# Attention inside a hybrid diffusion backbone: stacked query parts for the scores, values of two units at one visit, transposes behind the branch's weight products

## The reference, cut to what matters

```python
for l in range(DEPTH):                                   # DEPTH = 2
    hx = modulate(rms_norm(x, g_mix[l]), sh1, sc1)       # latent; hc the same of the context
    px = split_cols(hx @ w_in[l], IN_SIZES)              # q, k, v, conv, short conv, Fourier, 4 gates
    q = apply_rope(px[0].reshape(b, s, N_HEADS, HEAD_DIM), cos, sin)      # 8 heads of 64
    k = apply_rope(px[1].reshape(b, s, N_KV_HEADS, HEAD_DIM), cos, sin)   # 2 key heads
    y_attn = windowed_latent_attention(q, k, v, kc, vc, sink)   # window +-128, and all context keys
    m = sum(sigmoid(gate_i) * (y_i @ w_br_i) for the four branches)
    x = x + gt1 * (m @ w_out[l])
    # in layer 0 the context stream does the same, its queries reading the context keys alone
    x = x + gt2 * conv_ffn(...)                          # w_up, depthwise conv, silu, w_down
```

## Time and profile before

| | us |
|---|---|
| median of 3 runs (1251.46 to 1252.34) | 1252.09 |
| the profiled execution's own time | 1252.31 |
| its span, first to last instruction | 1250.5 |

### The profile page before, as it was taken

How to read it: one execution, slowest core, us unless ns; L and a number is a source line. 1 busy time by engine, 2 the same in 40 slices (tenths; PEclk the granted TensorE clock), 3 DMA queues, 4 the chain that set the end, 5 groups by cost and what they waited for, 6 DMA issues and landing times.

```text
span 1250.5 us, 19713 instructions
## 1 busy us (share of the span) xinstructions
PE 1241.1 (99%) x7504; PEld 1074.4 (86%) x7504; DVE 913.3 (73%) x1229; ACT 560.5 (45%) x912; POOL 340.7 (27%) x270
## 2 busy tenths in 40 slices
PE   8999999999999999999999999999999999999998
PEld 6788777787888898888888888899999999998996
DVE  4799889562898777662879674577897566778677
ACT  5223465653423345332223332344676645754554
POOL 1006699110143001111001110003693130144243
PEclk9999999999999999999999999999999999999999
DMA  9666422112466416562555664335433554556553
GB/s 380 221 214 197 147 65 71 65 54 99 143 191 227 136 61 203 186 225 80 182 166 188 212 194 145 122 119 189 150 123 118 175 178 138 186 185 207 180 170 116
DMA packets 52804, 200.33 MB, mean 160 GB/s; under 512 B 6001, under 2 KB 7921, under 8 KB 51569
## 3 DMA queue, kind: packets, MB, share of 16 engines
q1 hardware_dynamic: 52576, 199.13, 48.5%
q10 hardware_dynamic: 144, 0.07, 0.0%
HBM read 196.81 MB, written 1.05 MB: 158 GB/s over the span
## 4 chain that ended last, share of the span: by engine, by line
PE 97%; DVE 1%; ACT 0%; DMA 0%; issue 0%; DVEq 0%
PE psA L640 25%; PE psA L642 25%; PE psA L641 25%; PE psB L642 3%; PE psB L640 3%; PE psB L641 3%; PE psB L993 2%; PE psB L981 2%; PE psB L1140 2%; PE psB L1141 2%; PE psB L1142 2%; PE psA L968 1%; PE psA L646 1%; PE psA L651 1%; PE psA L647 1%; PE psB L675 1%
## 5 line engine op out<-in xcount | busy, mean ns | idle before, releaser
L640 PE MATMUL psA<-h_hi,w_hi 128*128 128x512 f32 (+1 forms) x1448 | 491.5, 339 | 0.1
L642 PE MATMUL psA<-h_hi,w_lo 128*128 128x512 f32 (+1 forms) x1448 | 488.0, 337 | 0.0
L641 PE MATMUL psA<-h_lo,w_hi 128*128 128x512 f32 (+1 forms) x1448 | 487.9, 337 | 0.0
L1196 ACT ACTIVATE w_hi<-raw 128x1024 fp32r<-128x1024 f32 (+2 forms) x246 | 274.2, 1117 | 278.0 <-PE psA L642 166.8
L1565 DVE TENSOR_TENSOR w_lo<-raw,w_hi 128x1024 fp32r<-128x1024 f32 (+2 forms) x246 | 339.4, 1380 | 61.5 <-ACT w_hi L1196 61.0
L640 PEld LDWEIGHTS psA<-h_hi,w_hi 128*128 128x128 f32 x1448 | 274.8, 190 | 29.9 <-DVE w_lo L1565 0.9
L642 PEld LDWEIGHTS psA<-h_hi,w_lo 128*128 128x128 f32 x1448 | 274.8, 190 | 29.1
L641 PEld LDWEIGHTS psA<-h_lo,w_hi 128*128 128x128 f32 x1448 | 274.9, 190 | 28.5 <-issue 0.2
L627 POOL TENSOR_TENSOR hid_lo<-sig,hid_hi 128x512 f32 (+3 forms) x44 | 68.6, 1558 | 441.5 <-ACT hid_hi L1513 441.5
L1597 DVE SCALAR_TENSOR_TENSOR ada_sum<-raw,csil,ada_sum 128x1024 f32<-128x1024 f32 x112 | 156.7, 1430 | 0.0
L2058 DVE SCALAR_TENSOR_TENSOR tmp<-psA,vec,tmp 128x510 f32<-128x510 f32 (+1 forms) x44 | 27.1, 615 | 68.3 <-ACT tmp L1524 68.1
(11 more groups left out here) (246 smaller groups left out, 1814.2 us busy)
## 6 DMA issues: line engine op xcount, KB each, us to landing
raw<-w_up SPq DMA_DIRECT2D x88, 512.0 KB, 4.3
raw<-w_ada SPq DMA_DIRECT2D x80, 512.0 KB, 3.5
raw<-w_in SPq DMA_DIRECT2D x35, 512.0 KB, 4.3
raw<-w_at SPq DMA_DIRECT2D x24, 512.0 KB, 3.5
raw<-w_dn SPq DMA_DIRECT2D x16, 704.0 KB, 5.2
raw<-w_dn SPq DMA_DIRECT2D x22, 512.0 KB, 3.5
raw<-w_fn SPq DMA_DIRECT2D x16, 640.0 KB, 4.1
raw<-w_sc SPq DMA_DIRECT2D x16, 640.0 KB, 3.9
```

Of the source, the lines that this page charges most:

```text
L640: pe.matmul(out, w0, hi, start=first, stop=False)
L641: pe.matmul(out, w0, lo, start=False, stop=False)
L642: return pe.matmul(out, w1, hi, start=False, stop=last)
L1196: act.activation(w_hi[:, s, 0:tiles * P], raw[:, r, 0:tiles * P], ACT.Copy).then_inc(head_done, 1)
```

## The change

The query's parts are stacked: `q_two` holds for each half of the heads the high part in that half's partitions and the low part in the other half's, and `k_two[half]` holds that half's high keys in both halves of the partitions. One matmul of 128 rows then gives q_hi k_hi + q_lo k_hi for a half; q_hi k_lo stays a pair of 64 rows. The band goes between the two kinds. ScalarE writes four copies of 64 partitions for the keys and two for each query; VectorE's subtractions become two of 64 partitions.

Values of units k-1 and k (k odd) are multiplied at one visit, with both units' weights side by side. The transposed weights lie in unused tails of the weight slots (layer 0) or in the context half of `h_hi` (layer 1). The results of two units are split by one instruction. In places below 16 the transposes come behind the branch's weight products, and ScalarE does the exponentials of a place before the copies of its transposes.

```diff
-        q_hi = place("q_hi", [2, P], F32R)
-        q_lo = place("q_lo", [2, P], F32R)
+        q_two = place("q_two", [2, 2, P], F32R)
...
-        k_hi = at("k_hi", [NT], F32R, sqa_off)
+        k_two = [at("k_two0", [NT], F32R, sqa_off), at("k_two1", [NT], F32R, t_off + 4 * NT * 2)]
+        prob_tails = at("prob_tails", [3 * SLOTS, SLOT], F32, base)[:, :, SLOT - P:SLOT]
+        prob_pair = at("prob_pair", [KD, NT], F32, h_off)[:, :, SEQ:NT]
...
+        def two_units(layer, y, unit):
+            _, qi, t = unit
+            if layer:
+                return y[:, 3 + t:5 + t, P * qi:P * qi + P]
+            return y[:, 4 + t, :].rearrange("p (s n) -> p s n", s=2)[:, :, P * qi:P * qi + P]
...
# TensorE, scores(k)
-                    pe.wait_ge(q_rest, b0 + k + 1)
+                    pe.wait_ge(q_rest, 2 * (b0 + k + 1))
                     b = (b0 + k) % 2
+                    for half in range(2):
+                        pe.matmul(score_bank(layer, half)[:, 0:nk * P], q_two[:, b, half, :],
+                                  k_two[half][:, k0 * P:(k0 + nk) * P], start=True, stop=False, skip_group_check=True)
                     if s == 0:
                         for half in range(2):
                             pe.matmul(score_bank(layer, half)[:, (1 - qi) * P:(2 - qi) * P], band[:, 2, :],
-                                      band[:, qi, :], start=True, stop=False, skip_group_check=True)
-                    for part, (qs, ks) in enumerate(((q_hi, k_hi), (q_hi, k_lo), (q_lo, k_hi))):
-                        for half in range(2):
-                            rows = slice(64 * half, 64 * half + 64)
-                            mm = pe.matmul(score_bank(layer, half)[:, 0:nk * P], qs[rows, b, :],
-                                           ks[rows, k0 * P:(k0 + nk) * P], start=(s == 1 and part == 0),
-                                           stop=(part == 2), skip_group_check=(s == 0))
-                            if part == 2:
-                                mm.then_inc(s_mm, 1)
+                                      band[:, qi, :], start=False, stop=False, skip_group_check=True)
+                    for half in range(2):
+                        rows = slice(64 * half, 64 * half + 64)
+                        pe.matmul(score_bank(layer, half)[:, 0:nk * P], q_two[rows, b, half, :],
+                                  k_lo[rows, k0 * P:(k0 + nk) * P], start=False, stop=True, skip_group_check=True)\
+                            .then_inc(s_mm, 1)
...
# TensorE, values(k)
+                    if k % 2 == 0:
+                        return
...
-                    for b in range(nk):
+                    for b in range(4):
+                        n = P if layer == 0 and b < 2 else 2 * P
                         for half in range(2):
-                            mm = pe.matmul(out_bank[64 * half:64 * half + 64, 0:P],
-                                           v[:, k0 + b, 64 * half:64 * half + 64],
-                                           probT[:, half, b * P:(b + 1) * P], start=(b == 0), stop=(b == nk - 1))
-                    mm.then_inc(o_mm, 1)
+                            if layer:
+                                prob = prob_pair[:, 4 * half + b, :]
+                            elif b < 2:
+                                prob = prob_tails[:, 6 * half + b, :]
+                            else:
+                                prob = prob_tails[:, 6 * half + b:6 * half + b + 3:2, :]
+                            mm = pe.matmul(out_bank[64 * half:64 * half + 64, 0:n],
+                                           v[:, b, 64 * half:64 * half + 64],
+                                           prob, start=(b == 0), stop=(b == 3),
+                                           skip_group_check=True)
+                    mm.then_inc(o_mm, 2)
...
# TensorE, attend(place), and at the end of merge
+                    if place >= 16:
+                        turn_place(place)
+
+                def turn_place(place):
                     for k, half in halves_at(layer, place, LATE[layer]["turn"]):
                         turn(k, half)
...
                     mm.then_inc(chunk_done, 1)
+                    if place is not None and place < 16:
+                        turn_place(place)
...
# ScalarE
-                    act.activation(q_hi[:, (b0 + k) % 2, :], q[:, t, q0:q0 + P], ACT.Copy).then_inc(q_head, 1)
+                    for half in range(2):
+                        rows = slice(64 * half, 64 * half + 64)
+                        act.activation(q_two[rows, (b0 + k) % 2, half, :], q[rows, t, q0:q0 + P], ACT.Copy).then_inc(q_head, 1)
...
-                act.activation(k_hi[:, :], k_all[:, :], ACT.Copy).then_inc(k_head, 1)
+                act.wait_ge(evac, n0 + 16)
+                for half in range(2):
+                    for into in range(2):
+                        act.activation(k_two[half][64 * into:64 * into + 64, :], k_all[64 * half:64 * half + 64, :], ACT.Copy)\
+                            .then_inc(k_head, 1)
...
# ScalarE, attend(place): attended, then
+                    for k, half in halves_at(layer, place, 0):
+                        weigh(k, half)
                     for k, half in halves_at(layer, place, LATE[layer]["turn"]):
                         turned(k, half)
-                    for k, half in halves_at(layer, place, 0):
-                        weigh(k, half)
...
# VectorE
-                dve.wait_ge(k_head, layer + 1)
-                dve.tensor_tensor(k_lo[:, :], k_all[:, :], k_hi[:, :].bitcast(F32), ALU.subtract).then_inc(k_rest, 1)
+                    for half in range(2):
+                        rows, others = slice(64 * half, 64 * half + 64), slice(64 - 64 * half, 128 - 64 * half)
+                        dve.tensor_tensor(q_two[others, (b0 + k) % 2, half, :], q[rows, t, q0:q0 + P],
+                                          q_two[rows, (b0 + k) % 2, half, :].bitcast(F32), ALU.subtract).then_inc(q_rest, 1)
+
+                dve.wait_ge(k_head, 4 * (layer + 1))
+                for half in range(2):
+                    rows = slice(64 * half, 64 * half + 64)
+                    dve.tensor_tensor(k_lo[rows, :], k_all[rows, :], k_two[half][rows, :].bitcast(F32), ALU.subtract)\
+                        .then_inc(k_rest, 1)
```

More of the change, by code:

```diff
@@ L275, in program @@
         k_lo = at("k_lo", [NT], F32R, k_off)
-        k_hi = at("k_hi", [NT], F32R, sqa_off)
+        k_two = [at("k_two0", [NT], F32R, sqa_off), at("k_two1", [NT], F32R, t_off + 4 * NT * 2)]
         x_in = at("x_in", [KD, NT], F32, q_off)
+        prob_tails = at("prob_tails", [3 * SLOTS, SLOT], F32, base)[:, :, SLOT - P:SLOT]
+        prob_pair = at("prob_pair", [KD, NT], F32, h_off)[:, :, SEQ:NT]
+        assert all(KD * P <= n * P <= SLOT - P for name, n in (("fn", SIZE[START["fn"]]), ("sc", SIZE[START["sc"]]), ("at", SIZE[START["at"]])))
         ada_first = at("ada_first", [FIRST_SLOTS, KD, 2 * P], F32, y_off)
@@ L952, in scores @@
                     if k == 0:
-                        pe.wait_ge(k_rest, layer + 1)
+                        pe.wait_ge(k_rest, 2 * (layer + 1))
                         pe.wait_ge(v_done, layer + 1)
@@ L985, in values @@
                 def values(k):
[L986 to L987 removed]
+                    if k % 2 == 0:
+                        return
                     pe.wait_ge(pt, 2 * (b0 + k) + 2)
[L989 to L991 removed]
+                    if b0 + k > 1:
+                        pe.wait_ge(o_rest, b0 + k - 1)
+                    for b in range(4):
+                        n = P if layer == 0 and b < 2 else 2 * P
                         for half in range(2):
[L993 to L996 removed]
+                            if layer:
[9 more added lines that the diff above has]
+                    mm.then_inc(o_mm, 2)
                 def attend(place):
@@ L1394, in turned @@
                     act.wait_ge(t_mm, 2 * b + half + 1)
-                    if b:
-                        act.wait_ge(o_mm, b)
-                    act.activation(probT[:, half, 0:wide(layer, k)], turn_bank(layer, half)[:, 0:wide(layer, k)], ACT.Copy)\
+                    if b > 1:
+                        act.wait_ge(o_mm, b - k % 2)
+                    n = wide(layer, k) // P
+                    if layer:
+                        into = prob_pair[:, 4 * half:4 * half + 4, k % 2 * P:(k % 2 + 1) * P]
+                    else:
+                        into = prob_tails[:, 6 * half + 4 * (k % 2):6 * half + 4 * (k % 2) + n, :]
+                    act.activation(into,
+                                   turn_bank(layer, half)[:, 0:n * P].rearrange("p (b n) -> p b n", b=n), ACT.Copy)\
                         .then_inc(pt, 1)
                 def attended(k):
-                    s, qi, t = un[k]
-                    c0 = SEQ * s + P * qi
-                    act.wait_ge(o_mm, b0 + k + 1)
-                    act.activation(y_hi[:, 4 + t, c0:c0 + P], out_bank[:, 0:P], ACT.Copy)\
-                        .then_inc(o_head, 1)
```

(16 more changed lines are left out.)

5 lines of the change are left out of this document (1 added, 4 removed).

## The result

| | before | after |
|---|---|---|
| median, us | 1252.21 (6 runs, 1251.46 to 1253.94) | 1262.11 (6 runs, 1260.55 to 1262.58) |
| ratio, 95% interval | 1 | 1.0076 [1.0065, 1.0086] |
| profiled execution, its span, us | 1252.31, 1250.5 | 1261.99, 1260.2 |

The change costs 9.9 us, 0.8%; the range reached only to 1254.4. TensorE's list of waits answers to the earlier trace rows and already names the places. Columns: engine, tile and line, what it waited for, us in total, times, longest. It is the whole list but one, 0.4 us on a DMA at the start.

The account below looks back on a forecast made before the run. TensorE, busy 99% of the span, was taken to bound the kernel. From 1252.31, less 1.16 gained on TensorE, plus 1.5 at layer 1's start, adjusted to the median and for joined passes: 1252.3 us, range 1249.9 to 1254.4.

Parts of the forecast that it names:

- Stacked products at 0.23: TensorE's scores: two products filling all 128 rows run one after the other, 0.23 us each; scores sum to 0.88, unchanged.
- the pair at 0.42: TensorE's scores: the remaining pair of 64 rows takes 0.42 us from its start to the next product.
- joined passes at half the cost of two: TensorE's values: one matmul over two units streams as long as the two did, 0.22 us; only fixed visit cost goes.
- first transposes behind the products without a switch: TensorE: transposes behind the weight products keep the full shape and pay no switch, 0.11 us each, the first too.
- no wait for the scaled weights: Layer 1: TensorE's 0.40 us wait for the scaled weights goes, as the transposes come 0.7 us later.
- the exponentials covered: ScalarE's exponentials wait for later transposes, but have about 4 us to spare in layer 0 and 2 in layer 1.
- The faster rival: A fixed cost goes with every matmul removed: 1250.5 us, or 1247.9 at about 60 cycles each; chance 0.10.
- The start of layer 1: Before layer 1's first scores, extra key copies and half ops make TensorE wait 1.5 us in the open.
- The upper bound, 2.8: Start of layer 1: the added wait reaches 2.8 us if each half op meets GpSimd.
- In layer 0 the same edit is covered: Start of layer 0: query's low parts ended two microseconds before the first score; extra ops are 0.63 and some 0.6.
- short by up to 0.6: Start of layer 0: if the extra ops met GpSimd twice, the cover would fall short by up to 0.6 us.
- The rival "VectorE falls behind": Layer 0: a second low-part op per place makes VectorE late; at 1.0 a pair it costs 3 us, 1255.3; chance 0.09.

Follow-up runs that it names:

- e1: The changed kernel without its stacked scores; scores and the splits of queries and keys as before, joined values and moved transposes kept: 1251.79 us, ratio 0.9993.
- e8: The changed kernel run once more, unaltered, for a second look at TensorE's clock: 1261.65 us, ratio 1.0073.
- e4: The changed kernel with 14 unused TensorE matmuls added just before it waits for layer 1's first scores: 1259.75 us, ratio 1.0057.
- e3: The kernel before, with only VectorE's subtractions for queries and keys cut into two ops of 64 partitions: 1257.03 us, ratio 1.0037.
- e5: The change with the stack turned round: one VectorE op per query, five ScalarE activations per query, two key copies instead of four: 1252.84 us, ratio 1.0000.
- e7: The changed kernel with ScalarE writing first the two key copies VectorE reads, then the two others from them: 1259.12 us, ratio 1.0054.
- e6: The changed kernel with GpSimd's convolution taps, all but each layer's first, over only 4 columns of each stream: 1254.61 us, ratio 1.0013.
- e2: The change's stacked scores and splits alone; values one unit a visit and transposes in mid-place as before: 1261.17 us, ratio 1.0074.
- e11: The kernel before with twelve idle times of TensorE forced into layer 0's up products by chains of activations: 1312.3 us in one run.

## Why the prediction was wrong

**Right.** Stacked products at 0.23, the pair at 0.42, so nothing from the scores; joined passes at half the cost of two; first transposes behind the products without a switch; no wait for the scaled weights; the exponentials covered. The faster rival, a fixed cost per matmul, does not show: 176 matmul records are gone, the scores take 0.88 without the band as before (160.57 to 161.67, less 0.22), and the joined values with the moved transposes gained 0.6 in e1, which is within the noise. By the Trainium skill, TensorEngine Tiling (Array Packing), Instruction Overhead, about 60 cycles for each of these matmuls would have been an estimated 4.4; the trace does not agree.

**The step that failed** is the pricing of VectorE's half ops, in three places, and it failed each time because I looked for one late thing and stopped.

1. *The start of layer 1*, a term of the sum that was mis-sized: 1.5 forecast, 2.9 measured. From TensorE's arrival, VectorE was to start the keys 0.39 before it and did so 0.01 behind it: half copies start 0.65 apart, not 0.52. Its two key ops took 1.61 and not 1.26, and the query's two needed ops 1.27 from start to end and not 0.68. The three differences, 0.40 + 0.35 + 0.59, are the miss. The 0.68 was the row of two whole ops one after the other. The upper bound, 2.8, was close, and something like it should have been the value, since GpSimd's taps run there too (from 889.6 on); but two ops of the 1.28 that it names would have given 3.4, so it was close in part by luck.
2. *"In layer 0 the same edit is covered", "short by up to 0.6".* The first scores are late by 0.56, so that bound was right. But I stopped at TensorE's next instruction. Behind the four ops on VectorE's queue stood the peak and, further on, the read of the modulation, for which TensorE waits at place 1: 1.4 more. I had asked for the steady places what stands behind the added op, and not here. And I took the list of waits as complete: the kernel before already waited 0.13 for this read at 148.52, too short for the list.
3. *The rival "VectorE falls behind"* had the mechanism, and 0.09. I put its worst at 0.4 per two places against a cover of 3.0, read at one place, 4. That 3.0 runs to VectorE's next peak (176.49), not to the scores, which began at 175.29. What counts is the time from the end of the branch sum to TensorE's first product into that bank, and it differs from place to place: before, it was 4.35 at place 4 (173.48 to 177.82), but 2.14 at place 7 and 2.59 at place 8 (211.43 + 0.69 = 212.12 to 214.70). Of the 2.59, 1.44 were the values and the transposes (213.26 to 214.70), which the change itself takes away from this place. After, 2.2 are left at place 4, 1.3 at place 5, 0.3 at place 7, and nothing at place 8. And places 5 and 6 carry a further op of the same kind, the low part of the short convolution, that I had not counted; it took 1.70 and 0.68 before, and 1.69 and 1.67 after.

**What was not in the sum at all** is the clock: three falls of 1.5 to 1.6 us in the profile of after. Before, TensorE had no idle time in the attention that could show it. A part of it replaces waits (e8): without any fall (e4) 7.4 of 10.0 us remain. So the main cause is the late VectorE. What is shown is that the half ops alone cost 4.7 (e3), that one whole op for a query, with two key copies fewer, brings all back (e5), that ScalarE's extra copies make 1.4 of the wait at layer 1's start (e7), and that the half ops are dear because of GpSimd's work (e6).

**What stays open.** Which idle times the clock answers to: it fell after 1.4, 1.6 and 2.9 us in the profile of after, not after 1.4 in e8, nor after 2.9 in e2, nor after the 1.6 at the start of the kernel before. Length alone does not decide; what else does stays open. Why e2 alone is nearly as slow as the whole change although its profile has no fall, I read from the waits on the weights at three places; it was not tried apart. Nor was it tried whether TensorE could wait for the modulation's read behind the scores of place 1 instead of ahead of them.

## What to carry to other kernels

Count instructions, not rows: an op that was cut in two halves over the partitions cost about twice, and where GpSimd was at work it paid that meeting twice. When an engine off the critical path is given more to do, follow its queue to every instruction for which the bottleneck engine waits, and take the cover at the tightest of the repeated places, in the schedule after the change. A wait too short for the list shows a place without cover. Give an expected stall of TensorE a second price, the clock it may lose behind it; it counts in full only where no late engine is met afterwards.

## What the runs showed of the hardware

- A VectorE subtraction of 64 x 128 took 0.29 us (median) with GpSimd's taps cut to 4 columns (e6) and 0.75 with them whole (after); the whole 128 x 128 op had a mean of 0.78 between 130 and 260 us before, and took 0.28 at its fastest. ScalarE's copies of 64 x 512 started 0.65 apart; behind a copy of 128 x 512 the next op started after 0.52.
- TensorE's granted clock fell from the 2.4 to the 1.2 GHz level after idle times as short as 1.4 us, in the profile of after when the engine was busy again, and not every time. Such a fall cost 1.5 to 1.6 us there. In e11 an idle time lost 1.7 or 3.4 us of clock, or none; of two of 2.5 us one had none.
- A slow clock in front of a late engine can be free: from 137.5 to 283.7 us the change lost 6.9 with two falls (after), 6.8 with one (e8, with 1.4 us more wait) and 5.3 with none (e4).
